# Prompt attention of a hybrid layer: search counts between score pieces and head copies, index scores one pair ahead, first loads in another order

## The chip, the cores and the metric

One core of a Trainium2 chip runs the whole program. Its five engines work side by side, each through its own list of instructions, and order themselves by semaphores: TensorE (PE, with its weight loads as PEld), VectorE (DVE), ScalarE (ACT), GpSimd (POOL) and SyncE (SP, which here only starts DMAs). The metric is the device time of one execution in microseconds, as the median of several runs.

## The reference, cut to what matters

The program is one trunk layer (projection, state space scan, sparse attention, experts) for a prompt of 2,048 tokens and a decode batch of 8 x 4 tokens. The change touches the prompt attention alone:

```python
def indexer_topk(q_idx, w_idx, k_idx, q_pos, topk):
    s = jnp.einsum('bthd,bsd->bths', q_idx, k_idx).astype(jnp.float32) * (IDX_DIM ** -0.5)
    score = jnp.einsum('bths,bth->bts', jax.nn.relu(s), w_idx.astype(jnp.float32)) * (IDX_HEADS ** -0.5)
    admissible = key_pos[None, :] <= q_pos[:, None]
    score = jnp.where(admissible[None], score, -jnp.inf)
    _, idx = lax.top_k(score, topk)
...
logits = jnp.einsum('btgrd,btkgd->btgrk', qg, k_sel).astype(jnp.float32) * (HEAD_DIM ** -0.5)
logits = jnp.where(valid[:, :, None, None, :], logits + bias, -jnp.inf)
p = jax.nn.softmax(logits, axis=-1).astype(v_sel.dtype)
o = jnp.einsum('btgrk,btkgd->btgrd', p, v_sel)
```

Each query attends to the 256 keys with the highest index score. There are 8 heads of 64, 2 key heads and 4 index heads. The kernel doesn't gather the selected keys: it attends to all earlier keys under a mask that is 0 for selected keys and -1e30 for the others.

## The kernel before

`attend_prompt` is a stage of its own between two barriers. The queries are cut into 16 tiles of 128 (`TILES`), and each tile into 4 pairs of heads (c and c + 4), so `order` has 64 pairs, numbered `u` = 0 to 63. A tile i attends to 128(i+1) keys. These are cut into `pieces` of up to 512 for the scores (the first one takes the remainder, so tiles 0 to 3 have one piece, tiles 4 to 7 two, 8 to 11 three, 12 to 15 four), and into `blocks` of up to 512 for the transposed probabilities.

What one pair does on each engine:

- PE, `scores`: for each piece two matmuls (e = 0, 1, one for each head) into one of two slots of the PSUM tile `SB`. A slot is free when what was in it two uses ago has been read (`free`, `before`). In the pass of pair u, PE issues pieces 0 and 1 of pair u+1, turns the first two blocks of pair u, issues piece 2 of pair u+1, turns the next blocks, and so on. `turn` transposes a block of the probabilities into `TB` (two buffers), `values` multiplies with V into `OB`.
- DVE, `pair`: for each piece and head one custom instruction (L2153, below "a maximum") that adds the mask, writes the logits to `L` and takes the row maximum. After the last piece a reduction (L2158) gives `nm`.
- ACT: `Exp` over the whole row for each head (L2002), then `Copy` of every turned block from PSUM to `PT` (L2014).
- POOL, `nearest`: adds the relative bias to the last 256 keys of the mask, two pairs ahead (`near_ok`). It also sends the reciprocal sums through DRAM and scales the finished tile.
- SP: queries and masks, two tiles ahead.

Two other jobs ride along.

The index scores and the search of tiles 12 to 15 (`GROUP` = 4 rows of the tile `sc`, 1,664 to 2,048 keys). In pairs 0 to 15 (`FIRST` = 16) every pair also computes one block of index scores: 4 matmuls (`index_half`, two halves that use `SB` slots), 4 `Relu` on ACT (`positive`), 4 multiply-adds on DVE (`index_scores`, L2039 and L2041). At u = 16 `sign` counts once over all four rows. Then 31 steps (`BITS`) of a search by bisection find the 256th largest score: DVE makes a candidate (`candidate`), rows 0 and 1 are counted on DVE (L2046), rows 2 and 3 on ACT (`Sign` with a sum, L1981), and `settle` takes the result once both are there (`acnt_ok`). The steps lie in pairs 17 to 43: two each in pairs 17 to 20, one in each later one. A pair's part of the loops, before:

```python
# ACT
if search_steps(u):
    count(search_steps(u)[0])            # both rows, before the pair's exponentials
...
# DVE
for step in search_steps(u)[0:1]:
    candidate(step)
...
pair(i, c)
if u < FIRST:
    index_scores(u)
for step in search_steps(u)[-1:]:
    settle(step)                         # its own two counts, then the wait for ACT
```

The sampled search, for the decode tokens: 32 counts (L2113) over `xs`, each summed over partitions by a small matmul (`sum_sampled`, L2250) whose result the next step reads. Before, there is one in each of pairs 32 to 63.

After pair 44 (`CUT`) come the threshold and the masks of tiles 12 to 15.

Of the kernel before, what the change touches and what calls it, by code (L numbers as in the profile page):

```python
# [6 lines left out]
F32 = mybir.dt.float32  # L7
# [3 lines left out]
ALU = mybir.AluOpType  # L11
# [4 lines left out]
P = 128  # L16
# [1758 lines left out]
def attend_prompt(nc, io, keep):  # L1775
# [5 lines left out]
    with Alloc(nc, "ap") as a:  # L1781
# [31 lines left out]
        par_in, bias_in, relu_ok, sc_ok, near_ok, masked = (a.sem(n) for n in ("par_in", "bias_in", "relu_ok", "sc_ok", "near_ok", "masked"))  # L1813
        mk_in = [a.sem(f"mk_in{i}") for i in range(2)]
        q_in = [a.sem(f"q_in{i}") for i in range(2)]
# [15 lines left out]
        def mask_of(i):  # L1831
            return mk[:, i % 2, 0:P * (i + 1)] if i < GROUP * H else row_of(i - GROUP * H)
# [14 lines left out]
        piece0 = [PAIRS * sum(len(pieces(j)) for j in range(i)) for i in range(TILES + 1)]  # L1847
        block0 = [2 * PAIRS * sum(len(blocks(j)) for j in range(i)) for i in range(TILES + 1)]
        order = [(i, c) for i in range(TILES) for c in range(PAIRS)]
# [4 lines left out]
        def use_piece(i, c, p):  # L1854
            q = piece0[i] + len(pieces(i)) * c + p
            u = PAIRS * i + c
            return q + 2 * min(u, FIRST)

        def use_half(n, half):
            i, c = order[n]  # L1860
            return use_piece(i, c, len(pieces(i)) - 1) + 1 + half

        def before(use):
# [5 lines left out]
            for i, c in order:  # L1869
                for p in range(len(pieces(i))):  # L1870
                    if use_piece(i, c, p) == use:
                        return ttr_ok, 2 * (piece0[i] + len(pieces(i)) * c + p + 1)


        STEP0 = [0] * (FIRST + 1)
        for u in range(FIRST, len(order)):
            STEP0.append(min(STEP0[-1] + (2 if FIRST < u <= FIRST + 4 else 1 if FIRST < u else 0), BITS))
        CUT = STEP0.index(BITS)

# [4 lines left out]
        def _(sp):  # L1884
            def queries(i):
                if i >= 2:
                    sp.wait_ge(ttr_ok, 2 * piece0[i - 1])
                sp.dma_start(qs[:, i % 2], io["qT"][:, :, i * P:(i + 1) * P].rearrange("c p t -> p c t")).then_inc(q_in[i % 2], 16)

            def mask(i):  # L1890
                if i >= 2:
                    sp.wait_ge(ttr_ok, 2 * piece0[i - 1])
# [10 lines left out]
            for i in range(1, TILES):  # L1903
                queries(i)
                if i < GROUP * H:
                    mask(i)
# [1426 lines left out]
```

## Time and profile before

| | |
|---|---|
| median of 3 runs | 3353.45 us (3343.98 to 3354.35) |
| the profiled execution | 3340.74 us |
| its span | 3338.9 us |
| mean granted TensorE clock | 0.907 |
| prompt attention, first instruction to last | 1091 us to about 1800 us |
| PE, DVE, ACT, POOL busy over the span | 83%, 48%, 31%, 24% |

The busy shares are means over stages with different limits. The prompt attention is some 709 us of the 3,339, it stands between barriers, and its time adds to that of the rest; so it is read by itself, stretch by stretch. The stretches below are cut at 1365.16, 1412.81 and 1516.96 us, where the first maxima reduction (L2158) of pairs 31, 35 and 43 starts. A number in brackets behind an instruction is the idle time of its engine just before it, and what ended it.

### The profile page before, as it was taken

Reading aid. Unit: us, or ns where it says so; the run is one execution under the profiler, and the core shown is the slowest. Engines: PE = TensorE matmul, PEld = TensorE weight load, DVE = VectorE, ACT = ScalarE, POOL = GpSimd, SP = SyncE. Lnnn points to the kernel's source line nnn. Section 1 sums busy time; section 2 is a strip of 40 time slices with the busy share of each in tenths; the row PEclk is TensorE's granted clock in tenths of the full one; section 3 lists DMA queues with packets and bytes.
Section 4 is the critical chain, followed back from the end, with each engine's and each line's share of the span. In section 5 each row is a group of like instructions: output and inputs, shape, how many; then the busy total and the mean of one; then the engine's idle time right before and its main releaser. Section 6 shows DMA issues by size and latency. Waiting matters only on the chain. (4 is left out here: it accounts for less than half of the span.)

```text
span 3338.9 us, 43104 instructions
## 1 busy us (share of the span) xinstructions
PE 2772.4 (83%) x14178; PEld 1354.7 (41%) x14179; DVE 1618.0 (48%) x3740; ACT 1038.2 (31%) x1887; POOL 814.7 (24%) x940
## 2 busy tenths in 40 slices
PE   7999998895966666777896879995999999999960
PEld 3545454352542234544564544442333333333320
DVE  1137377685866578878874434444111111111117
ACT  1123264464335458875564310110000000000002
POOL 1403131032550233222433310000221122122126
PEclk9999999997978778888998889996999999999985
DMA  6010101011341111100003846542787768877758
GB/s 209 27 52 20 67 13 42 28 37 52 111 122 57 56 34 42 37 23 14 17 14 129 249 137 203 182 144 106 264 299 265 266 227 299 300 277 252 269 188 337
DMA packets 239488, 456.08 MB, mean 137 GB/s; under 512 B 39212, under 2 KB 92958, under 8 KB 239342
## 3 DMA queue, kind: packets, MB, share of 16 engines
q1 hardware_dynamic: 195838, 334.50, 29.1%
q0 software_dynamic: 27872, 89.48, 8.6%
q10 hardware_dynamic: 15632, 30.29, 2.4%
q8 instruction: 75, 1.23, 0.2%
q14 instruction: 71, 0.58, 0.1%
HBM read 368.53 MB, written 85.65 MB: 136 GB/s over the span
## 5 line engine op out<-in xcount | busy, mean ns | idle before, releaser
L779 PE MATMUL pj_cm<-pj_xT,pj_w 128*64 128x512 f32 (+1 forms) x1216 | 395.2, 600 | 5.7 <-ACT pj_xst L677 3.2
L3042 DVE TENSOR_TENSOR ex_hid<-ex_sg,ex_pgu 128x256 f32<-128x256 f32 x83 | 35.0, 421 | 586.3 <-ACT ex_sg L3002 586.3
L3071 PE MATMUL ex_pgu<-pre_down_wgu,ex_xT 128*64 128x512 f32 x1312 | 293.5, 600 | 13.3 <-DVE ex_xT L3038 13.3
L3071 PE MATMUL ex_pgu<-ex_wgu,ex_xT 128*64 128x512 f32 x1344 | 297.7, 595 | 0.0
L2221 PE MATMUL ap_SB<-keep_kT,ap_qs 64*128 64x512 f32 (+3 forms) x640 | 176.5, 655 | 99.6 <-DVE ap_m L2153 70.6
L779 PEld LDWEIGHTS pj_cm<-pj_xT,pj_w 128*64 128x64 f32 (+1 forms) x1216 | 153.4, 163 | 239.9 <-issue 229.9
L2232 PE MATMUL ap_TB<-keep_const,ap_L 128*128 128x128 f32 x1088 | 179.9, 313 | 57.0 <-ACT ap_L L2002 41.1
L2014 ACT ACTIVATE ap_PT<-ap_TB 128x512 f32<-128x512 f32 (+3 forms) x320 | 155.2, 529 | 172.2 <-PE ap_TB L2232 171.5
L2232 PEld LDWEIGHTS ap_TB<-keep_const,ap_L 128*128 128x128 f32 x1088 | 136.0, 158 | 172.5 <-ACT ap_L L2002 84.5
L2994 POOL DMA_INDIRECT ex_xg<-xn,ex_cur x168 | 161.0, 959 | 104.2 <-issue 104.2
L703 ACT ACTIVATE se_U<-se_sc,se_cand 128x512 bf16<-128x512 f32 (+4 forms) x141 | 162.1, 1151 | 59.5 <-DVEq L525 59.3
L2002 ACT ACTIVATE ap_L<-ap_L,ap_nm 128x128 f32<-128x128 f32 (+15 forms) x128 | 153.0, 1198 | 65.5 <-DVE ap_nm L2158 61.3
L504 DVE TENSOR_SCALAR_CACHE_REDUCE se_U<-se_sc,se_cand 128x384 bf16<-128x384 f32 (+7 forms) x162 | 165.0, 1050 | 12.6
L3006 ACT ACTIVATE ex_hT<-ex_ph 128x256 f32<-128x256 f32 x83 | 31.8, 383 | 441.0 <-issue 440.0
L3071 PEld LDWEIGHTS ex_pgu<-pre_down_wgu,ex_xT 128*64 128x64 f32 x1312 | 91.4, 138 | 186.2 <-issue 172.5
L2991 POOL COPY ex_cur<-pre_rows 128x2 int32 x84 | 15.4, 183 | 617.6 <-DVE ex_xT L3038 617.5
L3071 PEld LDWEIGHTS ex_pgu<-ex_wgu,ex_xT 128*64 128x64 f32 x1344 | 93.1, 137 | 174.7 <-issue 174.7
L3002 ACT ACTIVATE ex_sg<-ex_pgu 128x256 f32<-128x256 f32 x83 | 31.8, 383 | 403.4 <-PE ex_pgu L3071 403.4
L2242 PE MATMUL ap_OB<-ap_PT,keep_V 128*64 128x128 f32 x2176 | 143.8, 289 | 15.4 <-ACT ap_PT L2014 15.3
L3087 PE MATMUL ex_py<-ex_wd,ex_hT 128*64 128x512 f32 x672 | 151.4, 592 | 2.3 <-ACT ex_hT L3006 2.3
L3087 PE MATMUL ex_py<-pre_down_wd,ex_hT 128*64 128x512 f32 x656 | 147.7, 592 | 0.0
L2046 DVE TENSOR_SCALAR_CACHE_REDUCE ap_marks<-ap_sc,ap_cand 128x1664 bf16<-128x1664 f32 (+1 forms) x72 | 143.3, 2029 | 0.9
(552 smaller groups left out, 4603.4 us busy)
## 6 DMA issues: line engine op xcount, KB each, us to landing
pre_down_wgu<-in_w_gate SPq DMA_DIRECT2D x16, 2048.0 KB, 9.0
pre_down_wgu<-in_w_up SPq DMA_DIRECT2D x16, 2048.0 KB, 14.8
pre_down_wd<-in_w_down SPq DMA_DIRECT2D x16, 2048.0 KB, 9.3
ex_wgu<-in_w_gate SPq DMA_DIRECT2D x16, 2048.0 KB, 9.0
ex_wgu<-in_w_up SPq DMA_DIRECT2D x16, 2048.0 KB, 14.8
ex_wd<-in_w_down SPq DMA_DIRECT2D x16, 2048.0 KB, 9.5
yslot<-ex_y ACTq DMA_DIRECT2D x166, 128.0 KB, 6.4
pj_x<-in_x_prompt SPq DMA_DIRECT2D x16, 512.0 KB, 5.1
```

The lines of the kernel that those rows point to most:

```text
L504: v.tensor_scalar(hits[s][:, 0:keys(h, s)], row_of(h, s), cand[:, s:s + 1].bitcast(F32), None, op, ALU.add, accum_out=cnt[:, s:s + 1])
L703: act_e.activation(hits[s][:, 0:keys(h, s)], row_of(h, s), ACT.Sign, bias=cand[:, s:s + 1].bitcast(F32), scale=-1.0, accum_out=cnt[:, s:s ...
L779: mm = pe.matmul(cm[u % 2][cols * n:cols * n + cols, 0:width_], w[:, k, c0:c0 + cols], xT[:, k, 0:width_], start=(k == 0), stop=(k == KD - 1))
L2002: s_.activation(L[:, u % 2, e, 0:n], L[:, u % 2, e, 0:n], ACT.Exp, bias=nm[:, h:h + 1], accum_out=rs[:, i % 2, h:h + 1]).then_inc(exp_ok, 1)
L2014: s_.activation(PT[:, e, o:o + w], TB[t % 2][:, 0:w], ACT.Copy).then_inc(pt_ok, 1)
L2046: v.tensor_scalar(hits[s][:, 0:keys(s)], row_of(s), cand[:, s:s + 1].bitcast(F32), None, op, ALU.add, accum_out=cnt[:, s:s + 1])
L2221: pe.matmul(SB[:, 2 * (use % 2) + e, 0:w], qs[hs, i % 2, c, :], keep["kT"][hs, o:o + w], start=True, stop=True).then_inc(s_ok, 1)
L2232: mm = pe.transpose(TB[t % 2][:, j:j + P], L[:, u % 2, e, o + j:o + j + P], ident)
L2242: mm = pe.matmul(OB[HD * e:HD * e + HD, P * c:P * c + P], keep["V"][:, kb, HD * e:HD * e + HD], PT[:, e, P * kb:P * kb + P], start=(kb == ...
L2994: pool.indirect_dma_start(xg[:, hh, :], None, quarters, bass.IndirectOffsetOnAxis(ap=cur[:, hh:hh + 1], axis=0)).then_inc(sm["xg_in"], 16)
L3071: mm = pe.matmul(pgu[BR * t:BR * t + BR, :], xT[:, k, :, :], wgu[par][:, k, :, 256 * t:256 * t + 256], start=(k == 0), stop=(k == KD - 1))
L3087: mm = pe.matmul(py[BR * t:BR * t + BR, :], hT[:, k % 2, k // 2, :], wd[par][:, k, 512 * t:512 * t + 512], start=(k == 0), stop=(k == 3))
```

## The change

- The first loads: the index queries of the first row come first, then queries and mask of tile 0, then the bias heads with a semaphore for each pair of them, where before POOL waited for all eight; the index queries have a semaphore for each row, where PE waited for all of them and for the bit table.
- The index scores are computed one pair ahead: block 0 before pair 0, and block u+1 after pair u. Each row's count for the sign follows when the row is ready (after pairs 2, 6, 10 and 14), and not all four at u = 16.
- The search begins in pair 15 (`BEGIN`): one step each in pairs 15 and 16, two each in 17 and 18, one in each of 19 to 43. It ends in the same pair as before.
- A step's two counts on DVE stand between the pieces of the scores: the first after piece 0, the second after piece 1. ACT makes its first count between the copies of the two heads of the pair before, and its second after them. The second step of pairs 17 and 18 keeps the old form.
- The sampled search begins at pair 36 and makes two counts in each of the last four pairs, the second between pieces 1 and 2.
- `TILE` lets tiles come in another order, but is the identity here.

```diff
+        BEGIN = FIRST - 1
+        STEP0 = [0] * (BEGIN + 1)
+        for u in range(BEGIN, len(order)):
+            STEP0.append(min(STEP0[-1] + (2 if BEGIN + 2 <= u < BEGIN + 4 else 1), BITS))
         CUT = STEP0.index(BITS)
+        SAMPLED = 36
+        SUM0 = [0] * (SAMPLED + 1)
+        for u in range(SAMPLED, len(order)):
+            SUM0.append(SUM0[-1] + (2 if u >= len(order) - PAIRS else 1))
...
# SyncE
+            index_queries(0)
             queries(0)
             mask(0)
-            for h in (0, 4, 1, 5, 2, 6, 3, 7):
-                sp.dma_start(bias[:, h, :], io["skew"][h, 0:P * 383].rearrange("(q c) -> q c", c=383)[:, 127:383]).then_inc(bias_in, 16)
+            for c in range(PAIRS):
+                for h in (c, c + PAIRS):
+                    sp.dma_start(bias[:, h, :], io["skew"][h, 0:P * 383].rearrange("(q c) -> q c", c=383)[:, 127:383]).then_inc(bias_in[c], 16)
             sp.dma_start(bits_i[:], io["bitrow"]).then_inc(par_in, 16)
...
# GpSimd
+                if u < PAIRS:
+                    pool.wait_ge(bias_in[c], 32)
...
-            pool.wait_ge(bias_in, 16 * HEADS)
...
# ScalarE
+            positive(0)
+            for u, (j, c) in enumerate(order):
...
+                if u + 1 < FIRST:
+                    positive(u + 1)
+                for step in search_steps(u)[1:]:
+                    s_.wait_ge(cand_ok, step + 1)
+                    count(2)
+                    count(3)
+                    s_.drain().then_inc(acnt_ok, 1)
+                turned(u, 0)
+                ahead = search_steps(u + 1)[0:1] if u + 1 < len(order) else []
+                for step in ahead:
+                    s_.wait_ge(cand_ok, step + 1)
+                    count(2)
+                turned(u, 1)
+                for step in ahead:
+                    count(3)
+                    s_.drain().then_inc(acnt_ok, 1)
...
# VectorE, in pair(), after a piece's two maxima
+                    if search_steps(u):
+                        if len(todo) == 1:
+                            count((0, 1), ALU.is_lt)
+                        elif p < 2:
+                            count((p,), ALU.is_lt)
+                    if p == 1 and SUM0[u + 1] == SUM0[u] + 2:
+                        sampled(SUM0[u] + 1)
...
+            index_scores(0)
+            for u, (j, c) in enumerate(order):
+                if SUM0[u + 1] > SUM0[u]:
+                    sampled(SUM0[u])
+                pair(j, c)
+                if u + 1 < FIRST:
+                    index_scores(u + 1)
+                    if u % PAIRS == PAIRS - 2:
+                        count((u // PAIRS,), ALU.is_ge)
                 for step in search_steps(u)[1:]:
                     settle(step - 1)
                     candidate(step)
+                    count((0, 1), ALU.is_lt)
                 for step in search_steps(u)[-1:]:
                     settle(step)
+                    if step + 1 < BITS:
+                        candidate(step + 1)
+                if u + 1 == BEGIN:
+                    sign()
+                    candidate(0)
...
# TensorE
+            index_half(0, 0)
+            index_half(0, 1)
...
+                if u + 1 < FIRST:
+                    index_half(u + 1, 0)
+                    index_half(u + 1, 1)
...
+                if ahead and SUM0[u + 2] == SUM0[u + 1] + 2:
+                    sum_sampled(SUM0[u + 1] + 1)
+                for (j2, c2), p in ahead[3:]:
+                    scores(j2, c2, p)
                 for e, k in turns[4:]:
-                    turn(i, c, e, k)
-                if 2 * FIRST <= u + 1 < len(order):
-                    sum_sampled(u + 2 - 2 * FIRST)
-                values(i, c)
+                    turn(j, c, e, k)
+                if ahead and SUM0[u + 2] > SUM0[u + 1]:
+                    sum_sampled(SUM0[u + 2])
+                values(j, c)
```

## Rows read from the trace of the kernel before

**Rows 1.** Stretches: us, each engine busy (instructions), PE clock, DMA share, GB/s

```profile
1091.00:1208.00 117.00, 79.02 (x418) 36.42 (x419) 75.20 (x179) 62.58 (x161) 43.44 (x71) 0.82 0.19 53
...
1217.00:1365.16 148.16, 98.09 (x660) 64.71 (x660) 123.06 (x287) 127.60 (x194) 47.85 (x80) 0.78 0.11 31
1365.16:1412.81 47.65, 35.27 (x262) 23.68 (x261) 39.07 (x102) 35.80 (x54) 12.51 (x21) 0.81 0.11 31
1412.81:1516.96 104.15, 76.78 (x594) 52.60 (x593) 83.04 (x211) 77.08 (x114) 24.97 (x42) 0.84 0.10 31
```

**Rows 2.** VectorE's waits, 1091 to 1208 us (total us, times, longest us)

```profile
DVE ap_sc L2039 <- ACT ap_rl L1976: 19.9, 12, 4.1
...
DVE ap_L L2153 <- POOL ap_last L1926: 8.2, 1, 8.2
```

**Rows 3.** VectorE's waits, 1217 to 1375 us

```profile
DVE ap_took L2062 <- ACTq L1983: 10.8, 8, 5.2
```

**Rows 4.** VectorE's waits, 1375 to 1517 us

```profile
DVE ap_took L2062 <- ACTq L1983: 9.6, 10, 1.8
DVE ap_L L2153 <- PE ap_SB L2221: 5.4, 10, 0.6
```

**Rows 5.** The start in order of time (start us, us, engine, line)

```profile
1092.22 4.35 SPq L1898 DMA_DIRECT2D ap_bias<-skew  x8
1093.83 0.51 PEld L2221 LDWEIGHTS ap_SB<-keep_kT,ap_qs 64*128 64x128 f32 x4 [21.65 <-DMA ap_qs<-qT]
...
1101.93 0.51 PEld L2210 LDWEIGHTS ap_SB<-keep_kiT,ap_qi 64*128 64x128 f32 x4 [7.59 <-DMA ap_qi<-qiT]
...
1104.67 0.48 DVE L2039 TENSOR_SCALAR ap_sc<-ap_rl,keep_widx 128x512 f32<-128x512 f32 x1 [4.11 <-ACT ap_rl L1976]
...
1108.16 0.29 DVE L2153 CUSTOM_DVE_ANT_0 ap_L<-ap_SB,ap_last 128x128 f32<-128x128 f32 x1 [0.19 <-issue]
```

**Rows 6.** A pair of tile 5 in order of time

```profile
1281.73 1.94 DVE L2046 TENSOR_SCALAR_CACHE_REDUCE ap_marks<-ap_sc,ap_cand 128x1664 bf16<-128x1664 f32 x1
...
1285.75 0.16 DVE L2062 TENSOR_TENSOR ap_took<-ap_cnt,ap_lim 128x4 int32<-128x4 f32 x1
...
1286.65 0.42 DVE L2153 CUSTOM_DVE_ANT_0 ap_L<-ap_SB,ap_mk 128x256 f32<-128x256 f32 x1
...
1289.57 1.08 PE L2221 MATMUL ap_SB<-keep_kT,ap_qs 64*128 64x512 f32 x4
...
1289.63 1.94 DVE L2046 TENSOR_SCALAR_CACHE_REDUCE ap_marks<-ap_sc,ap_cand 128x1664 bf16<-128x1664 f32 x1
```

**Rows 7.** A pair of tile 9 in order of time, three engines

```profile
1446.18 0.22 DVE L2127 TENSOR_SCALAR ap_dtook<-ap_CB,keep_const 128x1 int32<-128x1 f32 x1
...
1447.02 1.28 DVE L2113 TENSOR_SCALAR_CACHE_REDUCE ap_rl<-keep_xs,ap_dcand 128x1028 f32<-128x1028 f32 x1
...
1449.27 2.08 PE L2221 MATMUL ap_SB<-keep_kT,ap_qs 64*128 64x512 f32 x4 [1.32 <-DVE ap_m L2153]
...
1452.00 0.38 ACT L2014 ACTIVATE ap_PT<-ap_TB 128x256 f32<-128x256 f32 x1 [2.89 <-PE ap_TB L2232]
1452.70 1.51 ACT L2014 ACTIVATE ap_PT<-ap_TB 128x512 f32<-128x512 f32 x3 [0.32 <-PE ap_TB L2232]
1454.10 1.89 ACT L1981 ACTIVATE ap_marks<-ap_sc,ap_cand 128x1920 bf16<-128x1920 f32 x1
...
1458.12 0.17 DVE L2062 TENSOR_TENSOR ap_took<-ap_cnt,ap_lim 128x4 int32<-128x4 f32 x1 [0.91 <-ACTq L1983]
...
1462.45 0.40 PEld L2221 LDWEIGHTS ap_SB<-keep_kT,ap_qs 64*128 64x128 f32 x4 [1.93 <-DVE ap_m L2153]
```

**Rows 8.** Two pairs' first reductions in tile 15

```profile
1765.04 0.16 DVE L2158 TENSOR_REDUCE ap_nm<-ap_m 128x1 f32<-128x4 f32 x1
...
1777.30 0.16 DVE L2158 TENSOR_REDUCE ap_nm<-ap_m 128x1 f32<-128x4 f32 x1
```

**Rows 9.** VectorE's waits, 1740 to 1800 us

```profile
DVE ap_L L2153 <- PE ap_SB L2221: 7.9, 7, 2.6
```

More of the change, by code:

```diff
@@ L1910, in nearest @@
             def nearest(u):
-                i, c = order[u]
+                j, c = order[u]
+                i = TILE[j]
                 o, w = pieces(i)[-1]
@@ L1991, in _, with count, output @@
-            for u, (i, c) in enumerate(order):
-                n = P * (i + 1)
-                if search_steps(u):
-                    count(search_steps(u)[0])
-                for step in search_steps(u)[1:]:
-                    count(step)
+            def count(i):
+                s_.activation(hits[i][:, 0:keys(i)], row_of(i), ACT.Sign, bias=cand[:, i:i + 1].bitcast(F32),
+                              scale=-1.0, accum_out=cnt[:, i:i + 1])
+            def output(j):
+                s_.wait_ge(pv_ok, 2 * PAIRS * (j + 1))
+                if j >= 2:
+                    s_.wait_ge(att_st[j % 2], 16 * (j // 2))
+                s_.activation(ost[:, j % 2, :], OB[:], ACT.Copy).then_inc(ost_ok, 1)
@@ new lines, in turned @@
+            def turned(u, e):
+                j, c = order[u]
+                for k, (o, w) in enumerate(blocks(TILE[j])):
+                    t = block0[j] + (2 * c + e) * len(blocks(TILE[j])) + k
+                    s_.wait_ge(tp_ok, t + 1)
+                    if e == 0 and k == 0 and u:
+                        s_.wait_ge(pv_ok, 2 * u)
+                    s_.activation(PT[:, e, o:o + w], TB[t % 2][:, 0:w], ACT.Copy).then_inc(pt_ok, 1)
+            positive(0)
+            for u, (j, c) in enumerate(order):
+                n = P * (TILE[j] + 1)
@@ L2004, in _ @@
[L2004 to L2014 removed]
+                                  accum_out=rs[:, j % 2, h:h + 1]).then_inc(exp_ok, 1)
@@ L2048, in sign @@
             def sign():
-                count(range(GROUP), ALU.is_ge)
+                v.wait_ge(par_in, 16)
                 v.drain()
@@ L2058, in settle @@
             def settle(step):
-                count(range(MINE), ALU.is_lt)
                 v.drain()
@@ L2206, in index_half @@
                 use = use_half(n, half)
+                if kc == 0 and half == 0:
+                    pe.wait_ge(qi_in[s], 16)
                 free(use)
```

260 lines of the change are left out of this document (116 added, 144 removed).

## The prediction

> **What bounds the kernel now.** First read the small table: the prompt attention is one stage between barriers, so a microsecond saved in it is one saved in the whole, whatever PE's 83% says. Then read the stage by stretches [rows 1] and look, in each, for the engine whose busy time comes nearest to the stretch. In pairs 16 to 31 (to 1365.16) VectorE has 123.1 of 148.2 us and ScalarE 127.6; both are nearly full once the small gaps behind each instruction are counted. In pairs 36 to 43 (tiles 9 and 10) VectorE has only 83.0 of 104.2, ScalarE 77.1 and PE 76.8: nobody is full, so something goes round in a ring.
>
> Third, VectorE's waits. While the index scores are made it waits 19.9 us for the rectified scores and 8.2 once for the bias [rows 2]; from pair 17 to 31 it waits 10.8 us in 8 waits for ScalarE's counts, the longest 5.2 [rows 3]; in tiles 8 to 10 some 9.6 for the counts and 5.4 for score matmuls [rows 4].
>
> Last, the ring of tile 9, read in order of time [rows 7]. Piece 2's matmuls (1449.27) can start only when VectorE has read piece 0 and freed the slot. The turn of block 2 stands behind them on PE, so ScalarE's third copy starts at 1452.00 (2.73 us); copies to 1454.10 (2.10); both counts, until VectorE settles at 1458.12 (4.02); then candidate, sampled step and the next piece 0, until PE may start again at 1462.45 (4.33). That is 13.2 us for a pair; the stretch has 104.15 / 8 = 13.0 [rows 1]. VectorE's own work in such a pair is less. In tile 5 two counts take 4.02, settle and candidate 0.90, and the maxima of pieces of 256 and 512 keys 2.98 [rows 6]; of these a piece of 512 with its reductions has some 1.85, so one without has at most that, say 1.6. For tile 9: 4.33 + 4.02 + 1.6 + 1.85 = 11.8.
>
> **The start.** Now index block 0 begins on PE at 1101.93, held by its queries, and VectorE's first multiply-add is at 1104.67, 2.74 later [rows 5]. By then VectorE has idled 8.2 and 4.1 us [rows 2, 5]. After the change the index queries are the first load. The first load of now lets PE start at 1093.83; so index block 0 starts there, VectorE at 1096.6, and needs 3.5 us (1104.67 to 1108.16), to 1100.1. VectorE then idles 1096.6 - 1091.2 = 5.4 in place of 12.3: **6.9 us won**. Pair 0 needs the bias of heads 0 and 4: the bias loads are issued every 0.54 us from 1092.2 [rows 5], now 0.4 later, so the second is out by 1093.8, and with a load's three microseconds and POOL's add it is there before 1100. On SP the queries and mask of tile 0 come 0.4 us later, hidden by index block 0; the other index queries and the bit table are first needed pairs later. Bounds: 5 (all loads slower to land than the first one now) to 8.
>
> **Index scores one pair ahead.** From there the cycle is the same with another number: PE does index block, scores, turns, values; VectorE a block, a pair, a block, 16 blocks in both. The waits on rectified scores (19.9 less the first 4.1) stay. The sign counts are four of 2.0 us [rows 6] in both; at u = 16 they hold up everyone, and where they go they do too, for each stands ahead of the next pair's maxima. 0, bounds -2 and 2.
>
> **The search up to pair 31.** VectorE is the bound: in tile 5 the 7.90 us from count to count (1281.73 to 1289.63) are all its own work [rows 6]. Counts between pieces take none of this away; what can go is the 10.8 us of waits. With ScalarE one pair ahead, its counts are done before the exponentials of the same pair, and settle comes at least 2 us (a count) after these begin: nothing to wait for. The 5.2 goes because ScalarE's first count no longer stands behind a whole pair. A double pair keeps a second step in the old form, but ScalarE waits for that candidate with nothing ahead of it: some 0.3 each. **10.2 won**; bounds 0 (ScalarE, as full as VectorE, lags so far that settle waits) and 10.8. Behind ScalarE's new wait for the candidate stand the second head's copies, and PE's values and next scores behind them. The candidate is there 2.9 us after the last maximum (a count and 0.9), when ScalarE has just done two exponentials and the first head's copies.
>
> **Tile 8.** Its pairs take 47.65 / 4 = 11.9 us [rows 1], with a sampled step of 0.84 + 1.34 = 2.2 us in each [rows 7] that now comes in tile 9 and later. The ring without the step and with a piece 0 of 128: 2.73 + 2.0 + 4.0 + 1.85 = 10.6, less 0.3 (next part). At full clock the first term is 1.0 shorter, and VectorE's own work is 4.35 (maxima) + 4.02 + 0.90 = 9.3. Halfway between 9.3 and 10.3: 9.8, **8.4 won** in four pairs; bounds 6.4 and 10.4.
>
> **Tiles 9 and 10.** The third copy still waits for piece 2, the first count is still behind that copy, the second behind the other head's copies, and settle behind both: the same 2.73 + copies + 4.02 + 4.33. Only waits within the copies go (0.32 in the 2.10 [rows 7], since a turn can run under the first count). VectorE's counts move from beside ScalarE's counts to beside PE's turns, from one slack into another. So 12.5 for 13.0, **4 us won** in eight pairs; bounds 0 (the ring's 13.0) and 10.4 (VectorE's 11.7). The nearest row is the ring's.
>
> **Tile 15.** Four sampled steps more, 2.2 each. A pair takes 12.26 us [rows 8], and VectorE waits there for scores, 7.9 us in 7 waits, up to 2.6 [rows 9]. So they are mostly covered; but the second stands ahead of pieces 2 and 3, and in the last pair, where PE has no further scores to do, the exponentials start some 1 us late. **1.5 lost**, bounds 0 and 8.7 (all four, the cover gone).
>
> Tiles 11 to 14 keep their order. PE, POOL and the DMAs gain and lose no work.
>
> **Sum:** 6.9 + 10.2 + 8.4 + 4.0 - 1.5 = 28, less 1 for ScalarE's lag when tile 8's settle comes right behind the maxima: 27. From the profiled 3340.7 us that is 3314; but this execution lies 12.7 below the median of the runs shown and below all three, so the forecast is set against the median: 3353.4 - 27 = **3326 us**.
>
> One rule to weigh. ScalarE goes from `Copy` to `Sign` at 1454.10 without a gap [rows 7]. The Trainium skill (ScalarE: Activation LUTs, "What ACT_TABLE_LOAD costs") puts every switch to another table set at 2.66 us. The change makes two such turns between functions more in 27 pairs: by the rule, were they in different sets, an estimated 144 us lost; by the row, 0.
>
> **The rivals.**
>
> *The ring holds and tile 15 pays* (chance 0.17). Tiles 9 and 10 stay at 13.0 (-4), tile 8 at 10.3 (-2), the lag costs 2 more, and tile 15 pays 8.7 (-7). For: VectorE would have about 7 + 2 x 2.2 us of 12.26 there, with two waits for PE's sums inside. Against: the 7.9 us of waits. Gain 12: 3341.
>
> *All of VectorE's waits go* (0.08). Tiles 9 and 10 at 11.7, tile 8 at 9.3: 8.5 more, gain 36: 3318. It needs PE near full clock; now it has 0.81 to 0.84 [rows 1].
>
> *ScalarE becomes the bound in tiles 4 to 8* (0.11). It has 127.6 of 148.2 us [rows 1]; if its copies in two lots wait for a slow turn once more in each pair (0.8 us), 21 pairs give back 17: gain 10, 3343. Against: PE runs ahead under each count.
>
> *Slower: PE falls to half clock in the whole search* (0.07). Four score matmuls take 2.08 us in the ring and 1.08 in tile 5 [rows 6, 7]: the two levels, 1.2 and 2.4 GHz. Before the slow ones PE was idle 1.32 us. The change puts a count of 2 us into the middle of a pair's copies, and PE stands there. If the clock stays low for it, the scores and turns for which others wait cost 1.0 + 0.6 more in each of 28 pairs, 45 us against the 27: 3371. It decides from 0.97 us a pair. Against: at 0.78 in pairs 16 to 31 PE doesn't hold VectorE up. The Trainium skill (TensorE: Matmul & The Clock Gate, "Loop structure matters more than you think") speaks for this rival: matmuls with a long wait between them run cold.
>
> **How the numbers follow.** The remaining 0.57 is the forecast's own case, from a gain of 18 to one of 36 (3317 to 3335). The runs shown differ by 0.3% (10 us), about what a measurement can tell from no change. The 8 in 10 range goes from all waits gone, in an execution as fast as the profiled one (3306), to just behind ScalarE's case (3346). Faster by over 0.3%: forecast and first two rivals, 0.82. Within: 0.11. Slower: 0.07.
>
> **What would show it.** VectorE's first multiply-add near 1096.6; no wait for ScalarE's counts from pair 15 to 31 but some 0.3 in pairs 17 and 18; pairs of tile 8 at 9.8 us, of tiles 9 and 10 at 12.5 with ScalarE's third copy still waiting for PE; pairs of tile 15 at 12.3. The prediction is wrong if VectorE waits for scores in tiles 4 to 7, if pairs of tiles 9 and 10 come down to 11.7, or if PE's granted clock in the search falls well below 0.78.

## The result and the profile after

The changed kernel takes 3318.1 us (median of 4 runs, 3311.2 to 3321.2) against 3352.1 us for the kernel before: a ratio of 0.9911, 95% interval 0.9889 to 0.9933. The medians are 34.0 us apart, the ratio says some 30. The forecast was 3326 us in a range of 3306 to 3346. The profiled execution took 3318.59 us (span 3316.8, mean granted clock 0.913). Two slow executions of the experiments below, 3385.5 us of "POOL held back" and 13236.9 us of "POOL held back, sampled from 44", stand in no median or ratio.

Most of it is in the prompt attention. From VectorE's first instruction of the stage to its first of the next one are 714.05 us before and 684.80 after, 29.25 less. In the profiled execution the stage began 3.0 us later than before and what follows it took 4.2 us longer, so the two spans differ by 22.1. Below, the stage is the measure.

Stretches of the kernel after, cut where the first maxima reduction of pairs 15, 31, 35 and 43 starts (the third and fourth answer to the last two of [rows 1]); the fifth begins at pair 44's, the last is the whole stage. Columns: us, busy us and instructions of PE, PEld, DVE, ACT and POOL, granted clock, DMA share, GB/s.

```profile
1094.02:1208.11 114.09, 76.12 (x392) 34.31 (x392) 79.00 (x185) 61.67 (x157) 42.21 (x67) 0.84 0.17 49
1208.11:1353.66 145.55, 94.60 (x720) 64.46 (x722) 129.83 (x293) 131.64 (x206) 50.01 (x84) 0.84 0.13 36
1353.66:1394.63 40.97, 31.77 (x260) 21.36 (x258) 36.35 (x87) 36.25 (x56) 12.44 (x21) 0.90 0.13 37
1394.63:1495.14 100.51, 76.92 (x612) 55.43 (x610) 88.98 (x206) 77.29 (x115) 24.87 (x42) 0.87 0.11 32
1503.93:1778.82 274.89, 226.60 (x2071) 159.00 (x2069) 206.61 (x503) 153.44 (x241) 87.78 (x102) 0.91 0.06 16
1094.02:1778.82 684.80, 512.95 (x4096) 338.92 (x4096) 548.18 (x1294) 466.15 (x780) 219.42 (x320) 0.88 0.10 29
```

The same stretches of the kernel before, without tile 8's and tiles 9 and 10's, which [rows 1] has:

```profile
1091.02:1201.64 110.62, 74.32 (x404) 34.65 (x404) 70.23 (x170) 59.01 (x153) 41.18 (x67) 0.83 0.18 51
1201.64:1365.16 163.52, 105.42 (x696) 68.47 (x696) 136.78 (x306) 132.37 (x204) 50.11 (x84) 0.77 0.11 32
...
1530.32:1805.07 274.75, 226.91 (x2067) 157.77 (x2065) 199.64 (x483) 153.47 (x242) 87.76 (x102) 0.90 0.06 16
1091.02:1805.07 714.05, 529.01 (x4096) 343.89 (x4096) 539.29 (x1294) 467.69 (x780) 218.64 (x320) 0.85 0.10 28
```

Read the last row of each together. VectorE has 1294 instructions in both, so the work is the same. Its idle time fell from 714.05 - 539.29 = 174.8 us to 684.80 - 548.18 = 136.6. But its busy time rose, from 539.3 to 548.2: the same instructions became longer. That rise is the main thing the prediction did not have.

VectorE's waits after, in four stretches that answer to those of [rows 2, 3, 4, 9]: 1094 to 1208, 1208 to 1364, 1364 to 1495 and 1715 to 1775 us (total us, times, longest):

```profile
DVE ap_sc L2069 <- ACT ap_rl L1996: 21.3, 12, 4.6
DVE ap_sc L2071 <- ACT ap_rl L1996: 3.6, 7, 0.9
...
DVE ap_took L2091 <- ACTq L2044: 0.2, 1, 0.2
...
DVE ap_took L2091 <- ACTq L2044: 1.5, 3, 1.0
...
DVE ap_dtook L2156 <- PE ap_CB L2298: 2.5, 3, 0.9
...
DVE ap_L L2193 <- PE ap_SB L2267: 0.6, 1, 0.6
```

The wait for the bias is gone. Those for ScalarE's counts went from 10.8 us to 0.2 up to pair 31, and from 9.6 to 1.5 in tiles 8 to 10. In tile 15 the wait for scores went from 7.9 to 0.6. The waits for PE's sampled sums are 2.5 us there; in the window of [rows 9] they were 2.0.

The start, which answers to [rows 5]:

```profile
1093.94 0.37 SPq L1909 DMA_DIRECT2D ap_qi<-qiT  x1
...
1096.18 0.51 PEld L2256 LDWEIGHTS ap_SB<-keep_kiT,ap_qi 64*128 64x128 f32 x4 [20.92 <-DMA ap_qi<-qiT]
...
1098.92 0.49 DVE L2069 TENSOR_SCALAR ap_sc<-ap_rl,keep_widx 128x512 f32<-128x512 f32 x1 [4.62 <-ACT ap_rl L1996]
```

Last, where tile 9 begins, three engines in order of time. The end of this stretch answers to [rows 7].

```profile
1431.13 0.39 POOL L1945 COPY ap_last<-ap_mk 128x256 f32<-128x256 f32 x1 [8.93 <-DVE ap_m L2193]
...
1431.33 0.21 DVE L2091 TENSOR_TENSOR ap_took<-ap_cnt,ap_lim 128x4 int32<-128x4 f32 x1
1431.49 0.72 POOL L1946 TENSOR_TENSOR ap_last<-ap_mk,ap_bias 128x256 f32<-128x256 f32 x1
1431.61 0.63 DVE L2093 SCALAR_TENSOR_TENSOR ap_ub<-ap_took,ap_bits_i,ap_ub 128x4 int32<-128x4 int32 x1
...
1432.53 0.71 POOL L1946 TENSOR_TENSOR ap_last<-ap_mk,ap_bias 128x256 f32<-128x256 f32 x1
1432.70 0.22 DVE L2156 TENSOR_SCALAR ap_dtook<-ap_CB,keep_const 128x1 int32<-128x1 f32 x1
...
1433.21 1.25 POOL L1965 TENSOR_TENSOR ap_ost<-ap_ost,ap_R 128x512 f32<-128x512 f32 x1
1433.34 1.15 DVE L2150 SCALAR_TENSOR_TENSOR ap_dcand<-keep_ub,ap_bits_i,keep_xb 128x1 int32<-128x1 int32 x1
...
1436.83 1.13 PE L2267 MATMUL ap_SB<-keep_kT,ap_qs 64*128 64x512 f32 x4 [3.15 <-DVE ap_m L2193]
...
1438.53 0.38 ACT L2015 ACTIVATE ap_PT<-ap_TB 128x256 f32<-128x256 f32 x1 [3.69 <-PE ap_TB L2279]
1438.81 1.89 ACT L1999 ACTIVATE ap_marks<-ap_sc,ap_cand 128x1920 bf16<-128x1920 f32 x1
```

Look at the two long VectorE rows. `ub` has four elements in each partition and takes 0.63 us; `dcand` has one and takes 1.15. By these rounded times each ends 0.03 us after a POOL operation: 1431.61 + 0.63 = 1432.24 beside 1431.49 + 0.72 = 1432.21, and 1434.49 beside 1434.46. `dtook`, which reads PSUM and one constant, lies inside POOL's addition of 1432.53 and takes its 0.22. In pairs 15 to 43 of this trace 27 such small operations with two SBUF inputs take over 0.06 us more than alone, 12.8 us more in all, and every one of them ends 0.017 to 0.024 us after an operation of POOL. The ring of [rows 7] is still to be seen too: ScalarE's third copy waits 3.69 us for a turn that stands behind piece 2's matmuls.

### The profile page after: what moved, and what is told of

Same layout as the page of the kernel before. It is cut to its first block and busy times, and to the rows that moved or that the text cites. A ratio compares the mean times of both kernels' runs of the same rounds, so it can differ in the third digit from the quotient of the medians.

```text
span 3316.8 us, 43110 instructions
## 1 busy us (share of the span) xinstructions
PE 2759.5 (83%) x14178; PEld 1349.1 (41%) x14179; DVE 1629.8 (49%) x3740; ACT 1036.4 (31%) x1887; POOL 813.4 (25%) x940
## 3 DMA queue, kind: packets, MB, share of 16 engines
q1 hardware_dynamic: 195838, 334.50, 29.3%
## 5 line engine op out<-in xcount | busy, mean ns | idle before, releaser
L3093 DVE TENSOR_TENSOR ex_hid<-ex_sg,ex_pgu 128x256 f32<-128x256 f32 x83 | 34.9, 421 | 586.4 <-ACT ex_sg L3053 586.4
L2267 PE MATMUL ap_SB<-keep_kT,ap_qs 64*128 64x512 f32 (+3 forms) x640 | 164.7, 619 | 51.9 <-DVE ap_m L2193 43.2
L2279 PE MATMUL ap_TB<-keep_const,ap_L 128*128 128x128 f32 x1088 | 168.9, 298 | 45.0 <-ACT ap_PT L2015 42.1
L2290 PE MATMUL ap_OB<-ap_PT,keep_V 128*64 128x128 f32 x2176 | 152.6, 300 | 46.2 <-ACT ap_PT L2015 46.2
L2279 PEld LDWEIGHTS ap_TB<-keep_const,ap_L 128*128 128x128 f32 x1088 | 125.5, 149 | 149.5 <-issue 59.0
L2290 PEld LDWEIGHTS ap_OB<-ap_PT,keep_V 128*64 128x64 f32 x2176 | 135.2, 151 | 55.7 <-ACT ap_PT L2015 43.9
## 6 DMA issues: line engine op xcount, KB each, us to landing
pre_down_wgu<-in_w_up SPq DMA_DIRECT2D x16, 2048.0 KB, 14.9
```

The lines of the kernel that those rows point to most:

```text
L2267: pe.matmul(SB[:, 2 * (use % 2) + e, 0:w], qs[hs, j % 2, c, :], keep["kT"][hs, o:o + w], start=True, stop=True).then_inc(s_ok, 1)
L2279: mm = pe.transpose(TB[t % 2][:, at:at + P], L[:, u % 2, e, o + at:o + at + P], ident)
L2290: mm = pe.matmul(OB[HD * e:HD * e + HD, P * c:P * c + P], keep["V"][:, kb, HD * e:HD * e + HD], PT[:, e, P * kb:P * kb + P], start=(kb == ...
```

## The experiments

Each is an edit of the changed kernel, so its own place is beside that one. "Stage" is as above; busy and idle are VectorE's in the stage. "Behind" means VectorE's counts behind the pieces, "before the third copy" that ScalarE's first count stands there. The second to fifth row shared a chip, and so did the sixth to ninth and the tenth to twelfth, each time with runs of the kernel before.

| kernel | median us | ratio to before, 95% interval | stage | busy | idle |
|---|---|---|---|---|---|
| changed kernel | 3318.1 | 0.9911, 0.9889 to 0.9933 | 684.8 | 548.2 | 136.6 |
| the same once more | 3321.8 | 0.9922, 0.9904 to 0.9941 | 687.9 | 548.6 | 139.3 |
| VectorE's counts behind the pieces | 3309.2 | 0.9883, 0.9866 to 0.9899 | 674.7 | 534.7 | 140.0 |
| ScalarE's counts first | 3326.5 | 0.9942, 0.9922 to 0.9961 | 691.6 | 546.4 | 145.2 |
| count before the third copy | 3317.2 | 0.9914, 0.9897 to 0.9930 | 680.9 | 549.2 | 131.8 |
| POOL held back | 3309.7 | 0.9894, 0.9874 to 0.9913 | 673.3 | 533.2 | 140.1 |
| both engines' counts as before | 3324.0 | 0.9922, 0.9901 to 0.9944 | 687.9 | 534.6 | 153.4 |
| index queries loaded last | 3324.6 | 0.9930, 0.9913 to 0.9946 | 690.2 | 546.9 | 143.3 |
| sampled search from pair 32 | 3325.6 | 0.9943, 0.9926 to 0.9959 | 690.4 | 548.0 | 142.4 |
| behind, sampled from 44 | 3304.3 | 0.9890, 0.9854 to 0.9927 | 680.9 | 535.0 | 145.9 |
| the same, and before the third copy | 3304.2 | 0.9892, 0.9863 to 0.9922 | 674.2 | 534.5 | 139.7 |
| POOL held back, sampled from 44 | 3311.8 | 0.9909, 0.9883 to 0.9934 | | | |
| behind, and before the third copy | 3306.8 | 0.9877, 0.9858 to 0.9897 | 678.1 | 536.9 | 141.2 |

### The changed kernel once more

> The changed kernel once more, as the measure for the others. Stage (first VectorE instruction of the prompt attention to the first of the next stage) near 684.8 us, ratio to the kernel before 0.991. Both theories expect this.

The stage is 687.9, 3.1 us longer than in the first trace; 2.5 of it lies in tile 3 (34.9 us for 32.4), before the search. So the stage lengths of two single traces have to differ by more than about 3 us to mean something. A stretch without such a chance delay repeats better: tiles 9 and 10 take 100.2 us here and 100.5 there.

### VectorE's counts behind the pieces

```diff
-                    if search_steps(u):
-                        if len(todo) == 1:
-                            count((0, 1), ALU.is_lt)
-                        elif p < 2:
-                            count((p,), ALU.is_lt)
...
                 pair(j, c)
+                if search_steps(u):
+                    count((0, 1), ALU.is_lt)
```

> VectorE's two counts of a step come behind the pair's pieces again; ScalarE's counts stay where the change put them. My theory (VectorE is full in tiles 4 to 7, so the order of its own work gives nothing there; the gain is that settle no longer waits for ScalarE): pairs of tiles 4 to 7 as in the changed kernel (8.9 us mean), in tiles 8 to 10 VectorE waits up to 0.5 us more for a slot of piece 2, the stage 0 to 4 us longer. Rival (the counts between the pieces are what gives the gain, because they cover PE's and the slots' latencies): the stage is 10 us or more longer, with waits for PE at the maxima of tiles 4 to 10.

Neither: the stage is 10 to 13 us shorter, and the ratio 0.9883 against 0.9922 on the same chip, with intervals that don't meet. The part of the change that looked like a gain or nothing costs some 12 us. The stretch from pair 31 to 44 and the whole stage:

```profile
1354.09:1497.80 143.71, 112.08 (x932) 78.89 (x930) 125.49 (x317) 122.39 (x183) 39.60 (x67) 0.92 0.11 35
...
1098.16:1772.82 674.66, 510.32 (x4096) 338.10 (x4096) 534.65 (x1294) 465.45 (x780) 219.71 (x320) 0.88 0.10 30
```

VectorE's idle time is that of the changed kernel (140.0 beside 136.6 and 139.3); its busy time is 13.5 us less, with the same 1294 instructions. So it doesn't wait less: its instructions are shorter. Which ones, the groups of the changed kernel from pair 31 to 43 tell (busy us, mean ns, then idle):

```profile
L2093 DVE SCALAR_TENSOR_TENSOR ap_ub<-ap_took,ap_bits_i,ap_ub 128x4 int32<-128x4 int32 x12 | 5.8, 487 | 0.9
L2085 DVE SCALAR_TENSOR_TENSOR ap_cand<-ap_ub,ap_bits_i,ap_xb 128x4 int32<-128x4 int32 x12 | 5.0, 420 | 0.9
...
L2091 DVE TENSOR_TENSOR ap_took<-ap_cnt,ap_lim 128x4 int32<-128x4 f32 x12 | 3.6, 297 | 2.6 <-ACTq L2044 1.5 <-issue 0.4
```

With the counts behind the pieces the first two take 222 ns each and the third 163, as they do before the change (222, 210 and 162). POOL is released by the last maximum of a pair (`ttr_ok`) and then works for some 2.1 us. Before the change VectorE counts for 4 us at that time, and the counts are not longer for it: over 1,792 keys they take 2.07 to 2.08 us in both kernels. After it, settle and the candidate stand there.

### POOL held back

```diff
                     pool.wait_ge(ttr_ok, 2 * (piece0[j2] + len(pieces(TILE[j2])) * (c2 + 1)))
+                    if BEGIN <= u - 2 < CUT - 1:
+                        if STEP0[u - 1] < BITS:
+                            pool.wait_ge(cand_ok, STEP0[u - 1] + 1)
+                        if u - 1 >= SAMPLED:
+                            pool.wait_ge(part_ok, SUM0[u - 1] + 1)
```

> POOL begins its additions for pair u+2 only when VectorE has made the next candidate (in tiles 9 and 10 when it has also made the sampled count), in pairs 15 to 42; nothing else differs from the changed kernel. Seen so far: in the changed kernel VectorE's small operations of settle and candidate take 0.5 to 1.2 us in places where they take 0.16 to 0.22 in the kernel before, and POOL's copies, additions and multiplications stand at the same time. My theory (a small operation of VectorE with two inputs and a POOL operation hinder each other, and the counts between the pieces have put settle right where POOL is released by the last maximum): the long small operations are gone, tiles 8 to 10 lose 0.4 to 1.0 us a pair, the stage is 5 to 10 us shorter, about as much as with the counts behind the pieces. Rival (the small operations are long for another reason, say the place in the instruction list, or POOL is not the bound): they stay long, and the stage stays within 2 us of the changed kernel.

As the theory has it, and somewhat more: the stage is 11.5 and 14.6 us shorter, not 5 to 10. VectorE's order is untouched here; only POOL starts later. In order of time at the same place as above, and the two groups from pair 31 to 43:

```profile
1427.68 0.22 DVE L2098 SCALAR_TENSOR_TENSOR ap_ub<-ap_took,ap_bits_i,ap_ub 128x4 int32<-128x4 int32 x1
...
1428.84 0.22 DVE L2155 SCALAR_TENSOR_TENSOR ap_dcand<-keep_ub,ap_bits_i,keep_xb 128x1 int32<-128x1 int32 x1
...
1430.61 0.39 POOL L1950 COPY ap_last<-ap_mk 128x256 f32<-128x256 f32 x1 [8.35 <-DVE ap_rl L2147]
```

```profile
L2090 DVE SCALAR_TENSOR_TENSOR ap_cand<-ap_ub,ap_bits_i,ap_xb 128x4 int32<-128x4 int32 x12 | 2.7, 222 | 0.9
L2098 DVE SCALAR_TENSOR_TENSOR ap_ub<-ap_took,ap_bits_i,ap_ub 128x4 int32<-128x4 int32 x12 | 2.7, 222 | 0.9
```

```profile
1352.84:1494.34 141.50, 112.74 (x925) 78.85 (x925) 124.19 (x314) 120.71 (x182) 39.56 (x68) 0.92 0.12 37
1392.78:1485.56 92.78, 74.04 (x600) 52.83 (x598) 82.22 (x207) 76.55 (x115) 24.80 (x42) 0.90 0.11 35
```

Over the whole search the time that these small operations take above their undisturbed length falls from 12.8 us to 0.6, and the stage from 684.8 (687.9) to 673.3. Pairs 36 to 43 take 92.8 us for 100.5. This is the cause of the 12 us, shown from both sides: VectorE's small operations moved away from POOL, and POOL moved away from them. It is the traces that show it; the ratio of this kernel alone, 0.9894 (0.9874 to 0.9913), overlaps with those of the changed kernel. The Trainium skill (SBUF — State Buffer, "Who interferes with whom") states the rule: a VectorE instruction with two SBUF inputs contends with a GpSimd instruction that reads SBUF, for ports that one of them locks for itself. The trace agrees: `ub`, `cand`, `took` and `dcand` read two SBUF tensors and end 0.02 us after POOL's operation; the counts read one, `dtook` PSUM and a constant, and both are as long as ever.

The search is not the only place. The index multiply-adds (`sc` from `rl` and `sc`, both in SBUF) take 0.75 us alone and up to 2.6 beside POOL. With the plain multiplies before them (0.49 us alone, up to 2.64, though they read one SBUF tensor and a scalar) they lose 10.5 us in the kernel before and 7.1 in the changed one, and the small operations after pair 44 lose 3.5 and 3.9. No experiment held POOL back there.

### ScalarE's counts first, and both engines' counts as before

```diff
             for u, (j, c) in enumerate(order):
                 n = P * (TILE[j] + 1)
+                for step in search_steps(u)[0:1]:
+                    s_.wait_ge(cand_ok, step + 1)
+                    count(2)
+                    count(3)
+                    s_.drain().then_inc(acnt_ok, 1)
...
                 turned(u, 0)
-                ahead = search_steps(u + 1)[0:1] if u + 1 < len(order) else []
-                for step in ahead:
-                    s_.wait_ge(cand_ok, step + 1)
-                    count(2)
                 turned(u, 1)
-                for step in ahead:
-                    count(3)
-                    s_.drain().then_inc(acnt_ok, 1)
```

> ScalarE makes its two counts of a step before the pair's exponentials again; VectorE's counts stay between the pieces. My theory (ScalarE's place in the changed kernel removes the wait at settle): now the counts start only when the copies of the pair before are done, the waits for ScalarE's counts come back, some 0.3 to 0.5 us a pair in tiles 4 to 7 and 0.5 to 0.8 in tiles 8 to 10: the stage 6 to 14 us longer. Rival (VectorE's new order alone gives the gain): 0 to 2 us longer.

The stage is 3.7 and 6.8 us longer than in the two traces of the changed kernel, under and just above the theory's lower end of 6; the waits for ScalarE's counts from pair 15 to 44 come back as 12.4 us for 1.9. Both at once (this edit and VectorE's counts behind the pieces):

> Both engines' counts of a step stand where they stood before; the loads, the index scores one pair ahead, the early start of the search and the sampled schedule stay. My theory (ScalarE's place is what removes VectorE's waits for its counts, VectorE's new place costs by the meeting with POOL): VectorE's waits for ScalarE's counts come back in tiles 4 to 10, some 0.5 to 1 us a pair, the stage is 8 to 15 us longer than with only VectorE's counts put back (674.7), so 683 to 690. Rival (the place of the counts is worth little on either engine, the gain is loads and schedule): within 3 us of 674.7.

The stage is 687.9, 13.3 us longer than with VectorE's counts alone put back, as the theory has it. (The second step of the double pairs 17 and 18 stays where the change put it.) From pair 15 to 31 and from 31 to 44, and VectorE's waits over both:

```profile
1210.87:1355.04 144.17, 98.36 (x688) 67.57 (x688) 123.90 (x290) 129.49 (x200) 50.16 (x84) 0.79 0.12 37
1355.04:1512.90 157.86, 119.29 (x926) 79.94 (x925) 125.53 (x316) 122.79 (x182) 39.75 (x67) 0.85 0.11 32
```

```profile
DVE ap_took L2089 <- ACTq L2024: 15.1, 16, 1.5
DVE ap_L L2191 <- PE ap_SB L2262: 8.6, 13, 1.9
```

With VectorE's counts behind the pieces the same two stretches take 141.3 and 143.7 us. So ScalarE's place ahead is worth 2.9 us up to pair 31 and 14.2 from there to 44. And the two moves of counts together are worth about nothing: 687.9 with neither, 684.8 and 687.9 with both. What ScalarE's move wins, VectorE's move loses to POOL. The 26 us that this kernel is ahead of the one before come from the rest of the change: the start, the index scores one pair ahead, the earlier search with its double pairs, and the sampled schedule.

### Count before the third copy

```diff
             def turned(u, e, ahead=()):
                 j, c = order[u]
                 for k, (o, w) in enumerate(blocks(TILE[j])):
+                    if k == 2:
+                        for step in ahead:
+                            s_.wait_ge(cand_ok, step + 1)
+                            count(2)
...
+                early = len(blocks(TILE[j])) == 3
+                turned(u, 0, ahead if early else ())
+                for step in () if early else ahead:
                     s_.wait_ge(cand_ok, step + 1)
                     count(2)
```

> In tiles of three blocks (8 to 11; it matters in 8 to 10) ScalarE makes its first count ahead of the third copy, and no longer behind it. My theory (the ring of tiles 9 and 10 goes through the third copy and then the counts): the eight pairs from the reduction of pair 35 to that of pair 43 take some 11.7 us in place of 12.56, so the stage is 5 to 9 us shorter, and VectorE no longer waits for ScalarE's counts there. Rival (in the changed kernel those pairs are bound by VectorE's own work and the slower small operations between): within 1.5 us of the changed kernel.

The rival: pairs 36 to 43 take 98.99 us for 100.2 and 100.5, and the periods up to pair 39 are those of the changed kernel to the tenth (11.7, 12.0, 13.0). The stage is 3.9 and 7.0 us shorter than in the two traces of the changed kernel, but all beyond 1.2 to 1.5 us of it lies outside these pairs. What goes is most of VectorE's last 1.5 us of waits for the counts. The ring is there, but no longer than VectorE's own work.

### Index queries loaded last

```diff
-            index_queries(0)
             queries(0)
...
-            for s in range(1, GROUP):
+            for s in range(GROUP):
                 index_queries(s)
```

> The index queries are loaded last again, all else as changed. My theory (PE's index block 0 is held by its queries): VectorE's first multiply-add comes some 7 to 8 us later and the stage is 6 to 8 us longer. Rival (the loads' order is hidden, what counts is the smaller wait of POOL for the bias): 0 to 2 us.

PE's index block 0 starts at 1105.79, 8.3 us after the stage's first VectorE instruction, where it was 2.2. The first maxima reduction comes 5.9 us later (14.9 us after the stage's start for 9.0). The stage is 5.4 us longer than in the first trace of the changed kernel and 2.3 than in the second, which has its extra 2.5 in tile 3; the ratios say 3 to 6 us. VectorE's first multiply-add comes 6.2 us later. Where it acts, at the start, the order of loads is worth 5.9, a little less than the 6 to 8 of the theory.

### Sampled search from pair 32

```diff
-        SAMPLED = 36
+        SAMPLED = 32
...
-            SUM0.append(SUM0[-1] + (2 if u >= len(order) - PAIRS else 1))
+            SUM0.append(SUM0[-1] + 1)
```

> The sampled search runs once in each of pairs 32 to 63 as before, all else as changed. My theory: tile 8 gets its four steps of 2.2 us back, 7 to 9 us more, tile 15 loses the four second steps, 1.5 to 3 us less: the stage 5 to 7 us longer. Rival (tile 8 is held by a ring of PE and ScalarE, in which the steps of 2.2 us hide): the stage is equal or up to 3 us shorter.

From the reduction of pair 31 to that of pair 35 it takes 48.4 us for 41.0, so 7.4; tile 15 takes 48.3 for 51.4, but the end after it 28.2 for 26.3: 1.2 less there. That is 6.2. The whole stage is 5.6 and 2.5 us longer than in the two traces of the changed kernel, and the ratios say 7 to 11.

### Three kernels with the sampled search from pair 44

```diff
-        SAMPLED = 36
+        SAMPLED = 44
...
-            SUM0.append(SUM0[-1] + (2 if u >= len(order) - PAIRS else 1))
+            SUM0.append(SUM0[-1] + (2 if u >= 49 and order[u][1] else 1))
```

VectorE's counts stand behind the pieces in the first two of them, and POOL is held back in the third.

> VectorE's counts behind the pieces, and the sampled search begins only at pair 44: one step in each of pairs 44 to 63 and a second one in twelve of pairs 49 to 63 (in place of one from pair 36 and four second ones). My theory: with the counts behind the pieces tiles 9 and 10 (11.6 to 12.0 us a pair) are set by VectorE's own work and by a ring that also holds the sampled step, so all 2.2 us of it go: 16 to 18 us less there; in tiles 12 to 15 VectorE waits 16.6 us for scores, which covers half of the eight more second steps: 8 to 12 us given back. The stage is 5 to 9 us shorter than 674.7. Rival (VectorE's slack in tiles 12 to 15 is not where the second steps stand, and they delay the exponentials): all 17.6 us are given back, the stage is within 2 us of 674.7 or longer.

The rival. Pairs 36 to 43 take 82.6 us for 93.5, which is 10.9 less and not 16 to 18, and from pair 44 on:

```profile
1475.19:1768.02 292.83, 228.84 (x2086) 161.73 (x2084) 220.50 (x541) 154.04 (x241) 87.86 (x102) 0.91 0.05 15
```

```profile
DVE ap_dtook L2156 <- PE ap_CB L2295: 13.9, 12, 2.4
DVE ap_L L2193 <- PE ap_SB L2264: 6.9, 7, 2.1
```

That is 17.8 us more than 275.0, for eight steps of 2.2. VectorE's wait for scores did fall, from 16.6 us to 6.9, but a second step in a pair waits for a sum that stands in PE's list behind turns and scores: 13.9 us for 3.4. The slack was used up by the new wait.

> The same, and ScalarE's first count comes ahead of the third copy in tiles of three blocks. My theory: the ring through the third copy is as long as VectorE's own work once the sampled step is gone (both some 9.6 us), so breaking it gives little: 0 to 3 us beside the kernel without it. Rival (the ring alone holds tiles 9 and 10 at over 10.5 us a pair): 6 us or more shorter than the kernel without it.

The stage is 6.7 us shorter, as the rival has it, but the two medians are equal (3304.3 and 3304.2), so this rests on one trace of each. Pairs 36 to 43 take 78.2 us for 82.6, and VectorE's waits there for scores and for ScalarE's counts go from 6.6 us to 0.2: without the sampled steps the ring through the third copy does bind, for some 4.4 us. Tile 8 takes 37.3 us for 38.2, but that is its first period (9.35 for 10.25), in which the edit changes nothing yet. PE's granted clock in tiles 9 and 10 is 1.00 there, 0.94 with the ring.

> VectorE's counts between the pieces as in the changed kernel, POOL held back until the candidate is made, and the same later sampled search. My theory: as with the counts behind the pieces, since both only keep POOL away from the small operations: the stage within 3 us of that kernel. Rival (the place of the counts has a worth of its own once the sampled steps are gone from tiles 9 and 10): more than 4 us apart from it, in either direction, and the difference lies in tiles 9 and 10.

There is no trace of this kernel that can be set beside the others, so only times stand: 0.9909 against 0.9890, with intervals that overlap. It does not decide between the two.

### Counts behind the pieces, and before the third copy

This is the edit of VectorE's counts and that of the third copy together.

> VectorE's counts behind the pieces, ScalarE's first count ahead of the third copy in tiles of three blocks, the sampled search as in the changed kernel: meant to be the best of what was learnt. My theory: in tiles 9 and 10, with the sampled steps back, VectorE's own work sets the pair (11.7 us), so breaking the ring gives what it gave in tile 8 (0.9 us) and little else: the stage 672 to 674, ratio to the kernel before 0.986 to 0.989. Rival (the ring is worth the same 5 us here as without the sampled steps): stage 669 to 670.

The ratio, 0.9877 (0.9858 to 0.9897), lies in the expected range, beside 0.9883 for the kernel without the second edit. The stage, 678.1, is longer than both theories have it. Pairs 36 to 43 take 95.2 us for 93.5, and tile 8 38.2 for 38.2: with the sampled steps there, breaking the ring gives nothing. Five of these kernels stand at ratios of 0.988 to 0.989, some 6 to 15 us ahead of the changed kernel's two; the intervals don't rank them. The simplest, VectorE's counts put back and all else as changed, is the one to keep.

## Why the prediction came out, point by point

The first maxima reduction of a pair now comes after one (tiles 4 to 7) or both (tiles 8 to 10) of VectorE's counts of 2.0 us, so stretches that begin or end in the search are compared with that taken off.

| step | predicted | measured | the same with POOL held back |
|---|---|---|---|
| start: VectorE's idle time in the first block and pair | 12.3 to 5.4 | 12.3 to 5.2 | |
| stage start to pair 31 | 17.1 | 14.5 + 2.0 = 16.5 | 17.6 + 2.0 = 19.6 |
| tile 8 | 8.4 | 6.7 + 2.0 = 8.7 | 7.7 + 2.0 = 9.7 |
| tiles 9 and 10 | 4.0 | 3.6 | 11.4 |
| pair 43 to 44 | | 4.6 - 4.0 = 0.6 | 4.6 - 4.0 = 0.6 |
| pair 44 to the end | -1.5 | -0.1 | -0.5 |
| sum; the forecast takes 1 off for ScalarE's lag | 27 | 29.3 | 40.8 |

That 27 comes so near to 29.3 is partly luck. The last column is what the change is worth when POOL doesn't meet the small operations: 40.8 us. The forecast was 14 us too low on that, and the meeting with POOL, of which it had nothing, took 11.5 of them back.

- **The start: right.** PE's block 0 starts 2.2 us after the stage's first instruction, VectorE's first multiply-add 4.9 (5.6 predicted). The reversal gives it back.
- **The search to pair 31: the sum right, two parts of it wrong.** The waits for ScalarE's counts did go (10.8 to 0.2). The step "With ScalarE one pair ahead, its counts are done before the exponentials of the same pair" names the wrong cause for most of it: the kernel with both engines' counts as before is 17.6 us faster than the one before from the stage's start to pair 31, as much as the forecast's 17.1. From pair 15 to 31 it takes 144.2 us, only 2.9 more than with ScalarE ahead. Of the 10.8 us of waits before, 8.4 stood in the double pairs 17 to 20, one wait in each. They are gone in this kernel too, also in pairs 17 and 18, which are still double; it has waits of 5.3 us, all from pair 23 on. What changed in the double pairs is their form: before, VectorE settled the first step ahead of the pair's maxima, with ScalarE's counts of both steps ahead of its exponentials; now the first step is settled and the second made behind maxima and exponentials. So it isn't true that the second step "keeps the old form". No run takes this apart from the earlier beginning. And the step "Counts between pieces take none of this away" forgot the other side: by the meeting with POOL they add 4.1 us up to pair 31.
- **Tile 8: right in the number, partly by luck.** Its last three pairs take 10.4, 9.6 and 9.7 us for 9.8 predicted. The sampled steps are worth 7.4 of the 8.7. The 9.8 was halfway between a ring and VectorE's own 9.3. With POOL held back these pairs take 9.6, 9.2 and 9.2: VectorE's own work, and the rest was POOL.
- **Tiles 9 and 10: right number, wrong reason.** The step that failed is "the same 2.73 + copies + 4.02 + 4.33", from which comes "So 12.5 for 13.0". The 2.73, from PE's piece 2 to ScalarE's third copy, was mis-sized: it is 1.70 us in the pair shown (1436.83 to 1438.53) and 1.5 to 2.1 in all eight pairs of this trace (in the second trace one of them has 2.5), where in the kernel before six of the eight had 2.6 to 3.0. Piece 2's four matmuls take 1.13 us, their length at full clock, for 2.08; the stretch was granted 0.87 for 0.84. With 1.70, and without the 0.32 of waits within the copies, the prediction's own ring is 11.9 us, hardly more than VectorE's work of 11.7. (The step had a slip too: those 0.32 us alone make 12.7 of 13.0, and 2.6 us in eight pairs, not 4.) With POOL held back the pairs take 11.6 us, and VectorE waits 0.5 us for ScalarE's counts in all eight together; the disturbed small operations put them at 12.56. So the rival of 11.7 had the mechanism, and a loss that no rival had covered it up.
- **Tile 15: right.** Its pairs take 12.3 us from reduction to reduction, as predicted. The tile takes 51.4 us for 48.3, and the end behind its last reduction gives 1.5 of that back: 1.6 lost. Tiles 11 to 14 gave most of it back, in small amounts.
- **The index part: nearly right.** VectorE's idle time up to pair 15 fell from 40.4 to 35.1 us, the start's gain less some new waits; the waits on rectified scores themselves stayed, 19.9 and 21.3 us.
- **The rivals.** ScalarE did not become the bound (131.6 of 145.6 us up to pair 31, but VectorE waits 0.2 for it). PE did not fall to half clock: it was granted 0.84 for 0.77 from pair 15 to 31. ScalarE's additional turns from `Copy` to `Sign` cost nothing that shows, and not the estimated 144 us that the prediction weighed. No experiment drove the clock down, so what half clock would have cost stays open.
- **What no step had: 12.8 us lost to POOL.** The sentence "PE, POOL and the DMAs gain and lose no work" is true and not enough. POOL's work was the same, but VectorE's counts had covered it, and the change took the cover away. VectorE's busy time rose by only 8.9, since the index multiply-adds lost 3.4 us less to POOL than before.

## What to carry to other kernels

When an instruction list is reordered, look at what each moved piece was standing over: not only who waits for it, but which other engine works at that time and is released by the instruction before it. Compare the busy time of an engine with the same instruction count before and after: if it rose, look for groups with the same shape and a longer mean, and for the engine at work in the same microseconds. And a wait is slack only for work that waits for nothing itself: the second sampled steps filled VectorE's waits for scores and brought waits for sums.

## What the runs showed of the hardware

- VectorE operations on 1 or 4 elements a partition with two SBUF inputs, 0.16 to 0.22 us alone, took up to 1.19 us beside POOL, and all 27 lengthened ones of the search ended 0.02 us after an operation of POOL. VectorE's counts (one SBUF input, 2.0 us), its custom maxima (PSUM and SBUF, 0.69 us) and its small operations on PSUM were not longer beside POOL. The plain multiply of the index part (one SBUF input of 512 elements) was: up to 2.64 us for 0.49.
- It cost 12.8 us over the search: in tiles 8 to 10 some 0.4 to 0.9 us in most pairs, and 1.4 to 1.5 in the one pair of tile 9 and of tile 10 in which POOL also scales the finished tile (1.25 us).
- ScalarE's additional turns from `Copy` to `Sign` cost nothing that shows: the third copy starts at 1438.53 for 0.38 us and the count at 1438.81.
